# A chain of dense blocks on one core: the first two products in fp32 from the data as they land

## What is computed

```python
def conv_gdn_mixer(x, w_in, conv_a_w, conv_b_w, a_log, dt_bias, gdn_norm_g, w_out):
    ...
    proj = x @ w_in
    cuts = [wa, 2 * wa, 3 * wa, 4 * wa, 4 * wa + 3 * wg, 4 * wa + 4 * wg, 4 * wa + 4 * wg + h]
    h_a, c_a, b_a, z_a, qkv, z_b, beta_raw, a_raw = jnp.split(proj, cuts, axis=-1)
    ...
    qkv = jax.nn.silu(causal_depthwise_conv(qkv, conv_b_w))
    ...
    beta = jax.nn.sigmoid(beta_raw.astype(jnp.float32))
    g = -jnp.exp(a_log.astype(jnp.float32)) * jax.nn.softplus(a_raw.astype(jnp.float32) + dt_bias.astype(jnp.float32))
    o = gated_delta_rule(q, k, v, g, beta)
    ...
```

## Time and profile before

| | us |
|---|---|
| median of 3 timed runs | 1332.77 (1330.4 to 1337.19) |
| the profiled execution | 1327.51 |
| its span, first to last instruction | 1325.2 |
| TensorE busy | 1289.8 (97%) |
| VectorE busy | 955.5 (72%) |
| ScalarE busy | 738.3 (56%) |
| loads | 247.51 MB, 187 GB/s over the span |

### The profile page before, as it was taken

One profiled execution on the slowest core, in us unless ns is written; L12 is line 12 of the kernel. 1 busy time (PEld: TensorE's weight loads), 2 busy tenths in 40 slices (PEclk: granted clock), 3 DMA queues, 4 the chain that ended last, 5 costly groups with the idle time before them and its releaser, 6 DMA issues.

```text
span 1325.2 us, 30014 instructions
## 1 busy us (share of the span) xinstructions
PE 1289.8 (97%) x13136; PEld 1178.5 (89%) x13136; DVE 955.5 (72%) x1504; ACT 738.3 (56%) x993; POOL 25.5 (2%) x59
## 2 busy tenths in 40 slices
PE   6999999999999999999999998999999999999998
PEld 4999989899899999998988778888889898988887
DVE  4878868647468888887746977888677664887543
ACT  6667354465464565554554236777336783778431
POOL 0000000000000000000000000000000000000000
PEclk9999999999999999999999998999999999999999
DMA  6553545536276555654423244477764432575552
GB/s 268 177 174 131 222 192 193 195 125 250 93 282 228 198 218 208 219 212 160 145 79 128 98 160 170 181 292 295 294 236 155 159 128 96 194 276 198 190 191 64
DMA packets 34658, 247.51 MB, mean 187 GB/s; under 512 B 3872, under 2 KB 3872, under 8 KB 4960
## 3 DMA queue, kind: packets, MB, share of 16 engines
q1 hardware_dynamic: 29392, 209.16, 43.2%
q0 software_dynamic: 5136, 36.44, 7.6%
HBM read 244.53 MB, written 1.05 MB: 185 GB/s over the span
## 4 chain that ended last, share of the span: by engine, by line
PE 88%; DVE 5%; ACT 4%; issue 2%; DMA 0%; DVEq 0%; ACTq 0%
PE PS L502 15%; PE PS L418 11%; PE PS L419 10%; PE PS L420 10%; PE PS L503 8%; PE PS L517 7%; ACT WH L577 2%; DVE WL L590 2%; PE PS L434 2%; PE PS L435 2%; PE PS L436 2%; PE PS L1027 2%; PE PS L959 1%; PE PS L501 1%; PE PS L531 1%
## 5 line engine op out<-in xcount | busy, mean ns | idle before, releaser
L590 DVE TENSOR_TENSOR WL<-RAW,WH 128x2048 fp32r<-128x2048 f32 x166 | 380.0, 2290 | 108.5 <-ACT WH L577 105.0
L577 ACT ACTIVATE WH<-RAW 128x2048 fp32r<-128x2048 f32 x166 | 317.0, 1910 | 158.6 <-PE PS L503 70.0
L418 PE MATMUL PS<-XW,WH 128*128 128x256 f32 x992 | 291.2, 294 | 14.4 <-DVE WL L590 12.4
L419 PE MATMUL PS<-XW,WH 128*128 128x256 f32 x992 | 282.2, 284 | 0.0
L420 PE MATMUL PS<-XW,WL 128*128 128x256 f32 x992 | 282.1, 284 | 0.0
L418 PEld LDWEIGHTS PS<-XW,WH 128*128 128x128 f32 x992 | 191.5, 193 | 18.6 <-DVE WL L590 12.4
L419 PEld LDWEIGHTS PS<-XW,WH 128*128 128x128 f32 x992 | 191.9, 193 | 0.1
L420 PEld LDWEIGHTS PS<-XW,WL 128*128 128x128 f32 x992 | 191.7, 193 | 0.0
L502 PE MATMUL PS<-XW,WH 128*128 128x512 f32 x392 | 141.0, 398 | 0.2
L298 DVE SCALAR_TENSOR_TENSOR BIG<-BIG,C 128x256 f32<-128x256 f32 (+2 forms) x228 | 101.4, 507 | 32.8 <-ACT BIG L1390 13.5
L503 PE MATMUL PS<-XW,WL 128*128 128x256 f32 x392 | 110.0, 281 | 0.0
(11 more groups left out here) (405 smaller groups left out, 2545.6 us busy)
## 6 DMA issues: line engine op xcount, KB each, us to landing
RAW<-wst SPq DMA_DIRECT2D x196, 1024.0 KB, 4.8
BIG<-wad POOLq DMA_DIRECT2D x34, 1024.0 KB, 5.1
X<-xT SPq DMA_DIRECT2D x1, 1024.0 KB, 4.9
outT<-X SPq DMA_DIRECT2D x4, 256.0 KB, 4.3
K<-cst SPq DMA_DIRECT2D x1, 608.0 KB
CB<-crow SPq DMA_DIRECT2D x1, 512.0 KB
BIG<-pT POOLq DMA_DIRECT2D x2, 256.0 KB, 3.8
C<-cols SPq DMA_DIRECT2D x1, 370.0 KB
```

Source lines behind the costliest of these rows:

```text
L418: pe.matmul(o, h, hl[0][:, k0 + k, :], start=(k == 0), stop=False)
L419: pe.matmul(o, h, hl[1][:, k0 + k, :], start=False, stop=False)
L577: ac.activation(WH[p % NS][:, :], RAW[u % NR][:, :], ACT.Copy).then_inc(S.hi.tick(p), 1)
L590: ve.tensor_tensor(WL[p % NS][:, :], RAW[u % NR][:, :], WH[p % NS][:, :].bitcast(f32), ALU.subtract).then_inc(S.lo.tick(p), 1)
```

## The change

It has four parts.

1. **Loads.** x, unit 0 and unit 1 are loaded in halves, each half with its own semaphore: four of the eight k blocks of x, and the weight rows of four k. The order is x first half, unit 0 first half, x second half, unit 0 second half, then unit 1's halves. `cols` and `rows` now stand ahead of unit 2, `cst` and `crow` ahead of unit 3.
2. **Products 0 and 1** (`FIRST`) are made in plain fp32, straight from `X` and the RAW buffer, by the new `first_product`: 16 instructions each, k by k for both halves of the columns, waiting for the data of k = 0 to 3 and of k = 4 to 7 apart. Their units aren't split; units 3 and 4 go into `RAW0` and `RAW1` when the two products have read them. The slots start with unit 2.
3. **The gate product** stands after product 4 instead of 0, and its transposes after product 7 instead of 2, on all three engines.
4. ACT and DVE split one unit ahead of the twelve steps instead of three, and within a step DVE splits ahead of its part of the gates.

```diff
+FOLLOW = {("qkv", 0, 0): ("qkv", 0, 1), ("qkv", 1, 0): ("qkv", 1, 1),
...
+FIRST = (("qkv", 0, 0), ("qkv", 1, 0))
...
-        if spec is not None and key[0] in ("gate", "glu"):
+        if spec is not None and (key[0] in ("gate", "glu") or key in FIRST):
             direct[key] = len(units)
...
+        def first_product(pe, key):
+
+            u, b = direct[key], bank_of[key]
+            w = RAW[u][:, :].rearrange("p (k n) -> p k n", k=8)
+            vacate(pe, b, key)
+            for k in range(8):
+                if k % 4 == 0:
+                    if u == 0:
+                        pe.wait_ge(*S.x[k // 4]("in"))
+                    pe.wait_ge(*(S.raw[u](u) if k else S.first[u]("in")))
+                for n in range(2):
+                    t = pe.matmul(PS[b][:, n * T:(n + 1) * T], w[:, k, n * 128:(n + 1) * 128], X[:, k, :], start=(k + n == 0), stop=(k == 7 and n == 1))
+                    if k == 7:
+                        t.then_inc(S.mm.tick(key, n), 1)
...
-                    sp.wait_ge(*S.mm(key, 1 if key in OPENED else 0))
+                    sp.wait_ge(*S.mm(key, 1 if key in OPENED or key in FIRST else 0))
...
         def tensor_program(pe):
             for n in range(12):
-                product(pe, ("qkv", n % 3, n // 3), XHL, 0, (lambda k: pe.wait_ge(*S.al("x", k))) if n == 0 else None)
-                if n == 0:
+                if n < 2:
+                    first_product(pe, ("qkv", n, 0))
+                else:
+                    product(pe, ("qkv", n % 3, n // 3), XHL, 0, (lambda k: pe.wait_ge(*S.al("x", k))) if n == 2 else None)
+                if n == 4:
                     pe_gates1(pe)
-                if n == 2:
+                if n == 7:
                     pe_gates2(pe)
```

More of the change, by code:

```diff
@@ L61 @@
 SUM_BANK = {"r0": 3, "r1": 3, "r2": 3, "r3": 3}
-FOLLOW = {("gate", 0, 1): ("q", 0), ("gate", 0, 2): ("f", 0), ("gate", 0, 3): ("v", 0),
+FOLLOW = {("qkv", 0, 0): ("qkv", 0, 1), ("qkv", 1, 0): ("qkv", 1, 1),
+          ("gate", 0, 1): ("q", 0), ("gate", 0, 2): ("f", 0), ("gate", 0, 3): ("v", 0),
           ("glu", 5): ("co", 0), ("glu", 6): ("co", 1), ("glu", 7): ("co", 2)}
 LAST_FILL = [("zb", 0), ("oa", 0), ("oa", 1), ("oa", 2), ("oa", 3), ("zb", 1), ("zb", 2), ("zb", 3)]
+FIRST = (("qkv", 0, 0), ("qkv", 1, 0))
 LEVELS = 7
@@ L254, in program @@
         S.raw = [Signal(f"raw{i}", new(f"raw{i}")) for i in range(NR)]
-        S.x, S.inp, S.out = Signal("x", new("x")), Signal("inp", new("inp")), Signal("out", new("out"))
+        S.x = [Signal(f"x{i}", new(f"x{i}")) for i in range(2)]
+        S.first = [Signal(f"first{i}", new(f"first{i}")) for i in range(2)]
+        S.inp, S.out = Signal("inp", new("inp")), Signal("out", new("out"))
         S.p, S.late = [Signal(f"p{i}", new(f"p{i}")) for i in range(2)], Signal("late", new("late"))
@@ L618, in sync_program @@
         def sync_program(sp):
[L619 to L623, removed]
+            for h in range(2):
+                sp.dma_start(X[:, 4 * h:4 * h + 4, :], xT[:, 4 * h:4 * h + 4, :]).then_inc(S.x[h].tick("in", by=16), 16)
+                sp.dma_start(RAW[0][:, 1024 * h:1024 * h + 1024], wst[0][:, 1024 * h:1024 * h + 1024]).then_inc((S.raw[0].tick(0, by=16) if h else S.first[0].tick("in", by=16)), 16)
+            for h in range(2):
+                w = wst[1 if plan else 0]
+                sp.dma_start(RAW[1][:, 1024 * h:1024 * h + 1024], w[:, 1024 * h:1024 * h + 1024]).then_inc((S.raw[1].tick(1, by=16) if h else S.first[1].tick("in", by=16)), 16)
+            for u in range(2, len(units)):
+                if u in (2, 3):
+                    for i, (o, a) in enumerate((((C[:, :], cols), (R8[:, :], rows)), ((K[:, :], cst), (CB1[:, :], crow.broadcast_to([128, 1024]))))[u - 2]):
+                        sp.dma_start(o, a).then_inc(S.inp.tick(2 * u - 4 + i, by=16), 16)
                 if u - NR in ada_unit:
@@ L1763, in scalar_program @@
         def scalar_program(ac):
-            ac.wait_ge(*S.x("all"))
             for k in range(8):
+                if k % 4 == 0:
+                    ac.wait_ge(*S.x[k // 4]("in"))
                 ac.activation(XH[:, k, :], X[:, k, :], ACT.Copy).then_inc(S.ah.tick("x", k), 1)
-            for p in range(NS):
-                split_hi(ac, p)
+            split_hi(ac, 0)
             ac.wait_ge(*S.inp(3))
@@ L2572, in vector_program @@
                 ve.tensor_tensor(XL[:, k, :], X[:, k, :], XH[:, k, :].bitcast(f32), ALU.subtract).then_inc(S.al.tick("x", k), 1)
-            for p in range(NS):
-                split_lo(ve, p)
+            split_lo(ve, 0)
             for n in range(12):
                 ve_qkv(ve, n)
[L2577 to L2580, removed]
                 if n < 11:
                     then(ve, ("qkv", n % 3, n // 3))
+                if n == 4:
+                    ve_gates1(ve)
+                if n == 7:
+                    ve_gates2(ve)
             ve.wait_ge(*S.gate.ac("eg"))
```

## The result

The changed kernel is slower by half a per cent, where a gain of 4 us was forecast:

| | before | after |
|---|---|---|
| median of 19 runs each, taken in turn | 1331.33 (1327.33 to 1339.3) | **1338.57** (1335.75 to 1341.2) |
| ratio of the medians | | **1.0047**, interval 1.0035 to 1.0059 |
| the profiled execution | 1327.51 | 1340.15 |
| its span | 1325.2 | 1337.9 |

What follows compares the result with a forecast made beforehand. PE's own line was taken to bound the kernel (busy 1289.8 of 1325.2 us). Terms of -6.74, +2.32 and +0.15 made a 4.2 us gain: 1332.8 - 4.2 = 1328.6 us, range 1322 to 1334.

Steps and rivals of the forecast that it cites:

- Part 1: Kernel start: with halved loads PE's first matmul comes at 5.65 us instead of 12.39, 6.74 us earlier.
- rival (b): First loads: the pieces land together at 8.10, 2.45 us later, giving 1331.0 us; chance 0.06.
- Part 2: Products 0 and 1 in fp32: 14.00 us against 11.68 split, 2.32 us dearer.
- Rival (c): Products 0 and 1: fp32's four passes cost 4/3 of a split product, giving 1330.2 us; chance 0.03.
- Part 3: PE's first matmuls: 5.28 us at 1.2 GHz as before, losing 2.63 us instead of 2.48, 0.15 us dearer.
- Rival (e): Products 0 and 1: fp32 matmuls from idleness don't bring the clock up, +7.1 us, 1339.9; chance 0.03.
- Part 4: Product 2: its tile is split and ready at 18.7 us, 3.6 us before PE wants it at 22.3.
- rival (d): Load queue: each transfer pays its 2.36 us by itself, delaying product 2, +10.6 us, 1343.4; chance 0.02.
- Part 5: Fourth and fifth tiles load later; the fifth's low part is done at 31.3, wanted at 33.9, 2.6 us to spare.
- Part 6: Gate product and constants come later, with the same instructions and 7.01 us on PE; moved at cost 0.
- Rival (a): Body: 1.2 GHz stretches fall otherwise; without the longest 1325.2 us, chance 0.10; with another 1332.0, chance 0.08.
- The sum: Whole kernel: -6.74 + 2.32 + 0.15 gives a gain of 4.2 us, so 1327.51 - 4.2 = 1323.3 for the profiled execution.

Runs made afterwards that it cites:

- gates_late: The kernel before with only the gate product and its chain moved later on PE, ACT and DVE, as in the change; 1332.49 us, ratio 0.9996.
- tiny62: The changed kernel with 62 more PE instructions (2 semaphore increments, 15 tiny fp32 matmuls) hidden ahead of the first product; 1328.38 us, ratio 0.997.
- tiny318: The changed kernel with 318 more PE instructions (2 semaphore increments, 79 tiny fp32 matmuls) ahead of the first product; 1330.53 us, ratio 0.9973.
- tiny30: The changed kernel with 30 more PE instructions (2 semaphore increments, 7 tiny fp32 matmuls) ahead of the first product; 1330.98 us, ratio 0.9987.
- tiny94: The changed kernel with 94 more PE instructions (2 semaphore increments, 23 tiny fp32 matmuls) ahead of the first product; 1330.31 us, ratio 0.9993.
- tiny190: The changed kernel with 190 more PE instructions (2 semaphore increments, 47 tiny fp32 matmuls) ahead of the first product; 1330.57 us, ratio 0.9987.
- after_pad128: The changed kernel with 128 increments of an unused semaphore on PE ahead of its first matmul; 1349.93 us, ratio 1.0134.

## Why the prediction was wrong, point by point

- **Part 1, the start of PE**: 7.42 instead of 5.65, mis-sized by 1.8 us. Two pieces of 512 KB didn't land as one of 1024 does: ScalarE took the first half of x at 4.31, and PE had the first half of the tile at 7.42. The issues of the changed kernel (xcount, KB, median us to landing):

```profile
RAW<-wst SPq DMA_DIRECT2D x4, 512.0 KB, 8.2
X<-xT SPq DMA_DIRECT2D x2, 512.0 KB, 5.3
```

  It came between the forecast and rival (b), with 8.10.
- **Part 2, fp32**: held. The 32 instructions take 22.70 - 7.42 = 15.28 us; 14.00 at the forecast pace, and the rest is put down to the slow pace. Rival (c) is out.
- **Part 3, the slow pace**: it lasted 3.2 us instead of 5.28 (PE's pace doubles at 10.6), within the bounds given; it cost 15.28 - 14.00 = 1.28 us instead of 2.63 and so gave 1.35 of the 1.77 lost in Part 1 back. Rival (e) is out. Product 2 starts at 22.70; 22.3 was forecast.
- **Part 4**: the low part of product 2's tile is done at 20.2 instead of 18.7. No wait, and rival (d) is out.
- **Part 5**: the fifth tile landed at 27.8, its low part was done at 32.04 and product 4 wanted it at 34.3: 2.3 us to spare, 2.6 forecast.
- **Part 6**: `gates_late` shows the cost of 0, within its uncertainty.
- **The step that failed** is a sentence of the first part: that PE takes the others with it and "nothing behind it is tied to the start of the program". For data and semaphores that was right. But the borders of the instruction blocks are counted from the start of PE's program, so every instruction taken out at the start moves them through all that follows. In Part 2 the change of the number of instructions was worked out, and used for the price of two products alone. The sum, 1327.51 - 4.2, carried the whole body over unchanged; it has to have a term for it, which measures +10.7 us. The count above shows this step directly: the stops keep their place in the block and change their place in the work.
- **Rival (a)** named the place, the stretches at 1.2 GHz, but as a lottery: one more or one less, 3.4 us at most, for a shift in time. They aren't drawn by the time of the shift. In the changed kernel the loss belongs to its alignment and is there in all 19 runs: the fastest, 1335.75, is above the median of before, and the granted clock of all 19 is 0.985 to 0.989. What is chance from run to run, 1327 to 1339 in the kernel before, is there too, and that part of the rival stands.
- **What was to be seen beforehand.** The trace of before has "issue" with 2% of the chain, some 26 us, and stops of PE of 2 us with that releaser. They were passed over since nothing in the change touched them. It touched their place.

With the alignment of before the change is a gain: `tiny62` at 1328.38 is faster than both kernels, 0.997 of before (0.995 to 0.9991), and 10.2 us under the changed one. That it lies so near to the 1328.6 forecast is in part luck. `tiny318`, with the same alignment and start, is 2.2 us above it, and `tiny30`, `tiny94`, `tiny190` and `tiny318` gain 1.5 to 2.2 us on the kernel before, not 4.2.

## What to carry to other kernels

Count the instructions that an edit adds to or takes from an engine with long bursts of very short ones, and on an engine whose blocks hold 256, compare two kernels only with that number equal modulo 256; else a difference of under 1% can be the alignment and not the edit. When a kernel loses more than its waits explain, look in PE's timeline for "issue" stops inside such bursts and for half-clock stretches right behind them, and try a few free instructions at the start. A gain at the start is measured at a landmark behind it (here the taps of product 11) as well as at the end.

## What the runs showed of the hardware

- **Fetching instructions isn't free in bursts.** Stops of up to 3.2 us stand inside runs of 32x32 matmuls or up to a few us behind them, all 66 at the same place of a block of 256, and PE goes on 1.2 to 1.6 us after an instruction packet has ended. The DMA queues during the stop of `after_pad128`, 743.4 to 746.4 us (packets, MB, share):

```profile
q1 hardware_dynamic: 26, 0.08, 7.2%
q8 instruction: 1, 0.02, 2.0%
```

  The data queue is all but idle there (2% of 16 engines for 3 us are 0.96 us of one packet), so a crowded memory isn't needed for a stop. The Trainium skill, "Runtime: NRT & Kernel Launch", section Instruction fetch mechanics, says that instructions come in blocks of 16 KiB or 256 of them, which the 104 packets and 1.70 MB agree with. It calls the cost of a border mostly hidden; here most borders show no stop, but no kernel is without stops (3.0 to 9.6 us in all), and the two bad alignments cost 8 to 11 us more than that of before. Why a fetch comes late at one border and not at another, and what makes PE ask for the next block, no run shows.
- **The clock often falls behind a stop.** After a stop of 2.82 us, 10.24 us went at 1.2 GHz, after one of 2.08 us 6.82. Such a stop costs its length and half of the stretch behind it: 2.82 + 5.1, and 2.08 + 3.4. Not every stop is followed by one: the 2.02 us at 245.90 in the kernel before isn't.
- **An increment of a semaphore takes 0.15 us** on PE's sequencer: 62 moved the first matmul from 7.42 to 10.41 and 128 to 20.49: 66 more for 10.08 us, 0.153 each.
- **Two halves land later than one whole** at the start of the program: 1024 KB as two transfers (the first halves of x and of a tile) were used at 7.42 us (6.84 in `tiny62`), x as one transfer at 5.60.
